# Order of small VectorE steps and of w_mod loads in a two-block transformer kernel

## The reference

```python
# first block, layer l (l = 0 also carries 256 context tokens along)
h = rms_norm(x, g_pre_mix) * (1 + sc1) + sh1        # sh, sc, gt: six parts of silu(c) @ w_mod[l] + b_mod[l]
q, k = rope(h @ w_q), rope(h @ w_k); v = h @ w_v
o = diff_attend(q, k_all, v_all, lam)               # softmax - lam * softmax, 8 heads
y_a = silu(layer_norm(depthwise_conv(glu(h)))) @ w_conv_out
y_b = (rms_norm(o, subln_g) * (1 - lam_init)) @ w_attn_out   # norm over each head's 128 columns
y_c = (pool(h @ w_p) grouped) @ w_pool_out
y = (sig(g_a) * y_a + sig(g_b) * y_b + sig(g_c) * y_c) @ w_out
x = x + gt1 * rms_norm(y, g_post_mix)
x = x + gt2 * rms_norm(swiglu(rms_norm(x, g_pre_ffn) * (1 + sc2) + sh2), g_post_ffn)
```

## Time and profile before

| | |
|---|---|
| median of 3 runs | 2310.68 us (2307.33 to 2313.96) |
| the profiled execution | 2303.22 us, span 2301.4 us |
| granted TensorE clock, mean | 0.977 |
| PE busy | 2187.0 us (95%) |
| DVE busy | 1428.6 us (62%) |
| ACT busy | 887.3 us (39%) |
| POOL busy | 176.6 us (8%) |

### The profile page before, as it was taken

The page is one execution under the profiler, slowest core; times in us unless marked ns, Lnnn a source line. Parts: engine busy times, 40 slices in busy tenths (PEclk is TensorE's granted clock), DMA queues, the critical chain, the costliest instruction groups (busy, mean ns, idle before and its releaser), DMA issues. The chain is left out here.

```text
span 2301.4 us, 32565 instructions
## 1 busy us (share of the span) xinstructions
PE 2187.0 (95%) x12954; PEld 1866.4 (81%) x12954; DVE 1428.6 (62%) x2094; ACT 887.3 (39%) x1389; POOL 176.6 (8%) x251
## 2 busy tenths in 40 slices
PE   5999999999999999998999898999899999998998
PEld 3777667778888887788886897997788898897996
DVE  3487584754467756237957666864686565565664
ACT  3222373332342222235327445443545443344443
POOL 3412000000000000004310000000100000000000
PEclk8999999999999999999999999999989999999999
DMA  7544302333335566235421564766633566543663
GB/s 265 155 138 131 113 1 60 92 96 92 110 108 176 166 187 213 87 107 150 121 65 39 143 180 145 233 207 199 163 111 94 166 189 188 151 129 101 187 198 120
DMA packets 428651, 320.78 MB, mean 139 GB/s; under 512 B 25925, under 2 KB 379702, under 8 KB 428502
## 3 DMA queue, kind: packets, MB, share of 16 engines
q1 hardware_dynamic: 425408, 310.52, 45.1%
q0 software_dynamic: 2656, 8.03, 1.1%
q10 hardware_dynamic: 438, 0.17, 0.0%
HBM read 317.62 MB, written 1.05 MB: 138 GB/s over the span
## 5 line engine op out<-in xcount | busy, mean ns | idle before, releaser
L309 DVE TENSOR_TENSOR split<-raw,split 128x1024 fp32r<-128x1024 f32 x500 | 597.5, 1200 | 493.2 <-ACT split L306 488.5
L320 PE MATMUL PS<-HH,split 128*128 128x256 f32 (+1 forms) x2552 | 826.4, 324 | 39.2 <-DVE split L309 17.2
L321 PE MATMUL PS<-HL,split 128*128 128x256 f32 (+1 forms) x2552 | 811.8, 318 | 0.0
L322 PE MATMUL PS<-HH,split 128*128 128x256 f32 (+1 forms) x2552 | 811.2, 318 | 0.0
L306 ACT ACTIVATE split<-raw 128x1024 fp32r<-128x1024 f32 x500 | 506.8, 1026 | 457.4 <-PE PS L322 388.4
L320 PEld LDWEIGHTS PS<-HH,split 128*128 128x128 f32 x2552 | 488.4, 191 | 87.7 <-DVE split L309 21.3
L321 PEld LDWEIGHTS PS<-HL,split 128*128 128x128 f32 x2552 | 488.3, 191 | 35.9 <-issue 0.7
L322 PEld LDWEIGHTS PS<-HH,split 128*128 128x128 f32 x2552 | 487.7, 191 | 36.2
L320 PE MATMUL PS<-split,UH 128*128 128x512 f32 x416 | 167.4, 402 | 1.4 <-DVE split L309 1.4
L322 PE MATMUL PS<-split,UL 128*128 128x512 f32 x416 | 164.9, 396 | 0.0
L321 PE MATMUL PS<-split,UH 128*128 128x512 f32 x416 | 164.9, 396 | 0.0
(11 more groups left out here) (296 smaller groups left out, 2559.5 us busy)
## 6 DMA issues: line engine op xcount, KB each, us to landing
raw<-in_w_in_dram SPq DMA_DIRECT2D x120, 512.0 KB, 4.2
raw<-in_w_ffn_in_dram SPq DMA_DIRECT2D x88, 512.0 KB, 5.0
raw<-in_l_w_gate_up_dram SPq DMA_DIRECT2D x88, 512.0 KB, 3.9
G<-in_w_mod_dram SPq DMA_DIRECT2D x82, 512.0 KB, 4.1
raw<-in_w_ffn_out_dram SPq DMA_DIRECT2D x44, 512.0 KB, 3.5
raw<-in_l_w_down_dram SPq DMA_DIRECT2D x44, 512.0 KB, 4.6
raw<-in_l_w_in_dram SPq DMA_DIRECT2D x28, 512.0 KB, 4.0
raw<-in_w_attn_out_dram SPq DMA_DIRECT2D x16, 512.0 KB, 4.1
```

Of the source, the lines that this page charges most:

```text
L309: eng.tensor_tensor(c["low"], c["raw"], c["high"].bitcast(F32), ALU.subtract).then_inc(low_done, 1)
L320: pe.matmul(out, a[0], b[0], start=first, stop=False)
L321: pe.matmul(out, a[0], b[1], start=False, stop=False)
L322: return pe.matmul(out, a[1], b[0], start=False, stop=last)
```

## The change

Four edits, with no arithmetic changed.

1. DVE's wait for grid_rope moves from ahead of the GLU to just ahead of the rotations.
2. `head_norms` is cut into `head_squares`, `head_means` and `head_scales`. The list `others` gets two entries per token tile; the scaling of a tile goes into the entry with the next tile's squares, the last has an entry of its own.
3. A w_mod chunk of "L0_proj" is held and put into SP's list behind the next weight tile; held chunks don't count in "mods".
4. In `seam_dve` for two token tiles, both `by_rstd` are issued at step 2, where before the second stood at step 3, behind the first tile's `right_columns`.

```diff
+    held = []
-        def load(self, src, shape, split=True, ring="raw", home_free=None, split_home=None):
+        def load(self, src, shape, split=True, ring="raw", home_free=None, split_home=None, later=False):
-                 "mods": len(in_ring["mod"]), "home_free": home_free}
-            chunks.append(c)
+                 "mods": len(in_ring["mod"]) - len(held), "home_free": home_free}
+            if later:
+                held.append(c)
+            else:
+                chunks.append(c)
+                chunks.extend(held)
+                held.clear()
...
-                if 0 <= i - 2 < n:
-                    by_rstd(dve, name, i - 2)
+                if i == 2:
+                    for k in range(n):
+                        by_rstd(dve, name, k)
...
-            i, w = T.load(rows(A["w_mod"][l], k, 1, sec * D, D), (1, D), split=False, ring="mod")
+            i, w = T.load(rows(A["w_mod"][l], k, 1, sec * D, D), (1, D), split=False, ring="mod", later=phase != "start")
...
-            dve.wait_ge(S("grid_loaded"), 16 * (l + 1))
             last = [0] * NCH
...
             if l == 0:
                 lambda_sums()
+            dve.wait_ge(S("grid_loaded"), 16 * (l + 1))
             for i, rope in enumerate(ROPES):
                 rope_sin(*rope)
...
-            def head_norms(t):
+            def head_squares(t):
                 for o in range(2 * t, 2 * t + 2):
                     wait_read(dve, (L + "o", o))
                 dve_link(dve, dve.tensor_tensor(sq, O[:, t, :], O[:, t, :], ALU.mult))
+
+            def head_means(t):
                 dve_link(dve, dve.tensor_reduce(subs[:, 0, t, :], sq.rearrange("p (h d) -> p h d", h=HEADS), AX_X, ALU.add))
...
+            def head_scales(t):
                 dve.wait_ge(S(L + "o_rstd"), t + 1)
...
-            others += [[(head_norms, t)] for t in tiles]
+            for t in tiles:
+                others += [[(head_scales, t - 1)] * (t > 0) + [(head_squares, t)], [(head_means, t)]]
+            others.append([(head_scales, tiles[-1])])
```

## The result

The changed kernel took 2295.0 us in the median (2294.3 to 2298.0, 4 runs) against 2310.7 (2307.3 to 2314.0, 4 runs) for the kernel before beside it: ratio 0.9935, 95% interval 0.9922 to 0.9947, so 15.7 us less. The forecast against the median was 14.7 us less, 2296.0.

The account below looks back on a forecast made before the run. TensorE (PE), busy 2187.0 of 2301.4 us in fixed order, bounds the kernel, so only its stops can be won. Terms 1.8+2.0+9.1+0.8+1.0 = 14.7 us off the 2310.7 median give 2296.0 us, range 2286 to 2306.

Parts of the forecast that it names:

- Part 1: At the GLU's start, the first gate tile loads before the w_mod chunk, removing PE's 1.82 us stop; 1.8 us gained.
- Part 2: At layer 1's start, DVE splits earlier without the table wait, shortening PE's 5.09 us stop; 2.0 us gained.
- Part 3, layer 1: In layer 1's "ya" tiles, head norms in pieces remove most of 11.1 us excess; 9.1 us gained.
- the crumbs: In layer 1's "ya", small PE waits of 0.2 to 0.6 us would remain, about 2 us in sum, costing no clock.
- rival (a): Head-norm pieces still starve PE, three heavy steps costing 1.6 us more each; sum 9.9 us, 2300.8 us; chance 0.14.
- Layer 0: Layer 0's gate tiles gain 2.0 us from norms in pieces; the last scaling before OTH costs 1.2; net 0.8 us.
- The 1.7 for the clock: Layer 0's longer stop before OTH might bring the clock down, costing 1.7 us more.
- Part 4: In the layer-1 seam, the second tile is scaled 1.6 us earlier, of which 1.0 us reaches PE.
- (b): Short stops keep the lower clock in layer 1 and at layer 0's longer stop; sum 10.0 us, 2300.7 us; chance 0.13.
- The rule weighed: Frequent small idles between matmul groups make the clock swing between levels, so layer 1's small waits would lose full speed.
- (c): Gain nearly gone: rival (a) and (b) together and Part 2 halved; 4.2 us gained, 2306.5 us; chance 0.06.
- (d): w_mod chunks stuck behind a weight tile's slot come late, 22 times 1.5 us; slower, 2329 us; chance 0.05.

Follow-up runs that it names:

- table_only: The kernel before with only DVE's wait for the table (grid_rope) moved behind the GLU; 2310.19 us, 0.9988 of the kernel before.
- early_mem: Changed kernel with layer 0's first head-norm squares in the free earlier entry and layer 1's load of X issued after POOL's pooling; 2290.63 us.
- two_pieces: Changed kernel with each head norm in two pieces, not three: squares and means together, scaling one gate tile later; 2295.9 us, 0.9940 of before.
- hold4: Changed kernel with each w_mod chunk held behind four weight tiles, not one; 2297.6 us, 0.9950 of the kernel before.
- after_third: The changed kernel run again, unchanged, beside later variants; 2295.54 us, 0.9937 of the kernel before.

## Why the prediction came out

**The sum.** By the places in the traces: 2.1 (w_mod) + 1.5 (table, 1.95 less a mean of 0.5 given back) + 10.1 (layer 1's norms) + 1.0 (layer 0's) + 1.1 (seam) = 15.8 us, against 14.7 forecast and 15.7 measured. It holds because PE's order is fixed and each stop stands alone. The whole traces agree: PE stands still for 114.4 us before and for 102.0, 102.3 and 101.6 in the three of the changed kernel, 12.1 to 12.8 less; with the 3.4 of clock in "ya" that is 15.5 to 16.2. That the forecast came so near the median has a share of luck: one term was 0.5 too high, the others 0.1 to 1.0 too low, and all were added up from one execution of the kernel before that was 7.5 us under its median.

**Part 1**, 1.8 forecast: the stop at 73.63 is gone, and nothing stands in its place. From ACT's copy ahead of it to one behind it (64.10 and 91.49 before, 63.08 and 88.38 after) it is 27.39 and 25.30 us, 2.1 less, and 2.1 in the other two traces as well. SP's queue of the changed kernel: the first gate tile goes out at 43.57, 20 us before the chunk behind which it was queued, and the next one behind the chunk:
```profile
43.57 0.38 SPq L1952 DMA_DIRECT2D raw<-in_w_in_dram  x1
...
63.67 0.33 SPq L1952 DMA_DIRECT2D G<-in_w_mod_dram  x1
64.04 1.55 SPq L1952 DMA_DIRECT2D raw<-in_w_in_dram  x1
```
The single part's 0.14% (0.04 to 0.25) is 3.2 us and holds 1.8.

**Part 2**, 2.0 forecast, 1.95 at its own stop. The term was slightly too high because of a step that the prediction left near nothing: "the three raw tiles that SP may then fetch 2 us earlier meet other transfers". I priced the fetch at 5.4 us, from another stage, and allowed half to be given back. Beside the load of X it took 8.2 us in this trace, 8.4 in table_only. In table_only all was given back, below my lower end of 1.0. With that load moved away (early_mem) it took 4.2. Before, the weight tile's load was issued 3.2 us behind the load of X, now 1.3.

**Part 3, layer 1**, 9.1 forecast, 10.1 measured (8.6 if before has the shorter form of its second stop). The mechanism was right, the crumbs too dear: I took 2 us of them since DVE "starts about level"; the window has 27.59 us of PE in 27.80. DVE was not level but ahead, waiting for ACT when the norms began:
```profile
1298.69 0.69 DVE L315 TENSOR_TENSOR split<-raw,split 128x512 fp32r<-128x512 f32 x1 [1.02 <-ACT split L312]
```
The window with 0.2 us of standing still excludes rival (a). The same arithmetic of DVE steps against PE's 4.40 us gave 2.8 us of stops for two_pieces, where 3.8 came.

**Layer 0**, 0.8 forecast, 1.0 measured: from 433.30 to the first OTH matmul at 510.80 it was 77.50 us, from 430.27 to 506.76 it is 76.49. The tiles gave 2.2 (2.0 forecast), and behind them 31.92 us and not 30.77 were needed, 1.15 lost where 1.2 was forecast. The forecast put all of it into the OTH stop, to grow to 2.3 us; 0.8 stands there, and 0.16 in a new stop at 498.24, ahead of the transposes of the last scaled tile (PE reached the OTH stop 4.8 us earlier than before, DVE took up the splits 4.05 earlier, 498.10 for 502.15: DVE's merge ahead of them had itself come 5.2 us earlier, which paid for part of the scaling). The 1.7 for the clock was rightly kept out of the likeliest sum: it came in one trace of five.

**Part 4**, 1.0 forecast: the seam's stops went from 4.42+2.12+2.92 = 9.46 to 4.42+3.94 = 8.36, 1.1 less. What was late next was, as said, the second tile's highs and lows.

**The rivals.** (b), short stops keep the lower clock: not in "ya", where the clock was 1.00 in eight windows of eight. The rule weighed (the Trainium skill, "TensorE: Matmul & The Clock Gate", section "A second HAM failure mode: psum-queue depth-cycling") speaks of frequent small idles. No run here puts it to a hard test: the crumbs did not come, each of the eight windows has one stop over 0.1 us, of 0.2 to 0.5 us. That is no licence for short stops: the clock was at 0.63 after 2.47 us and at 0.72 after 1.83, though not each time. (c) falls with (a) and (b). (d) is no danger at one tile; at four it cost a few us.

## What to carry to other kernels

Where one engine's order is fixed and it is busy 95% of the time, price each of its stops by itself: they add up, and a helper engine's long job wants cutting to pieces shorter than one unit of the bound engine's work (the window of "ya" shows both its effects; that the finer pieces alone shorten the whole run is not shown). What is moved into an earlier place should be asked what it displaces: the last piece landed before a stage that had no slack, and a load met another load. To compare stages, cut windows between the same two matmuls in both traces; here they mostly repeat to 0.4 us, while whole executions of one kernel scatter by 4 to 13. And where each execution has its span and mean clock, split the time by them before calling two kernels equal.

## What the runs showed of the chip that was not expected

- The same 512 KB weight tile, where layer 1 begins, took 4.7 to 5.5 us from issue to landing in the four traces that issue it 2.9 to 3.2 us behind the load of X from mem, 6.7 to 9.1 in the eight that issue it 1.3 us behind, and 4.2 and 4.5 in the two with that load moved away.
- Stops of PE of 1.8 to 2.0 us were followed by half clock in three cases of eleven (one of five before OTH, two of four at the start, none of two in two_pieces); one of 2.67 us in hold4 was, too (0.83 over 10 us). A stretch of 230 us with PE busy for 99% of it had 0.98 in one execution and 0.95 in another.
- In whole executions the time at the lower level cost 50 to 67 us in 14 traces, most of it at places that no edit touched. This can make the several us by which executions of one kernel differ, but not all of them: outside the clock, too, the six executions of after_third scatter with a standard deviation of 3 us.
